# A three-block transformer kernel on one core: values made among the softmax units, head squares summed as heads come, branches of the last layer two blocks at a time

## The reference

```
# first block
x = x + 0.5 * rmsnorm(swiglu(rmsnorm(x)))
qkv = rmsnorm(x) @ w_qkv                      # 16 heads of 64: 8 "neighbourhood", 8 "dilated"
o_na, o_dil = rmsnorm(attention(...)), rmsnorm(attention(...))   # each over its 512 columns
x = x + rmsnorm(concat(o_na, o_dil) @ w_out)
x = x + 0.5 * rmsnorm(swiglu(rmsnorm(x)))
# layers l = 0, 1 (layer 0 also for a context of 256 tokens)
h = rms_norm(x) * (1 + scale) + shift          # scale, shift from (silu(c) @ w_mod + b_mod)
z = h @ w_in                                   # keys, values, forget gates, queries, branch gates
o_four, o_attn, o_hgrn = fourier(z), window_attention(z), gated_recurrence(z)   # 512 columns each
y = sum over the branches of sigmoid(gate_b) * (o_b @ w_branch_b)
x = x + m2 * (y @ w_out)
x = x + m5 * (relu(h2 @ w_ff1) ** 2 @ w_ff2)
```

## Time and profile before

| | us |
|---|---|
| median of 3 runs | 2107.01 |
| lowest, highest | 2104.97, 2107.38 |
| the profiled execution | 2112.87 |
| its span in the trace | 2111.0 |
| mean granted clock of PE in it | 0.984 |
| PE busy | 2013.7 |
| DVE, ACT, POOL busy | 1273.0, 946.5, 482.0 |

### The profile page before, as it was taken

How to read it: one execution, slowest core, us unless ns; L and a number is a source line. 1 busy time by engine, 2 the same in 40 slices (tenths; PEclk the granted TensorE clock), 3 DMA queues, 4 the chain that set the end, 5 groups by cost and what they waited for, 6 DMA issues and landing times.

```text
span 2111.0 us, 30414 instructions
## 1 busy us (share of the span) xinstructions
PE 2013.7 (95%) x12246; PEld 1761.6 (83%) x12246; DVE 1273.0 (60%) x1963; ACT 946.5 (45%) x1509; POOL 482.0 (23%) x293
## 2 busy tenths in 40 slices
PE   7999898899989999999999999999989899989999
PEld 6899876899978888787578788888878898688999
DVE  5679786578855772553864583254465946765410
ACT  5454434455447333423653442243265453655643
POOL 1201000000000000000034355455500000067887
PEclk9999998899999999999999999999999999999999
DMA  7987561366832212221023244466522333134554
GB/s 256 267 299 264 173 227 41 120 222 219 270 119 90 70 51 76 94 71 60 1 72 118 95 155 150 140 204 202 182 87 93 100 126 113 43 120 157 182 191 150
DMA packets 84636, 299.23 MB, mean 142 GB/s; under 512 B 9992, under 2 KB 13200, under 8 KB 84112
## 3 DMA queue, kind: packets, MB, share of 16 engines
q1 hardware_dynamic: 64512, 231.76, 32.4%
q0 software_dynamic: 17280, 60.95, 9.2%
q10 hardware_dynamic: 2704, 4.57, 0.6%
HBM read 296.18 MB, written 4.11 MB: 142 GB/s over the span
## 4 chain that ended last, share of the span: by engine, by line
PE 79%; DVE 9%; ACT 5%; DMA 3%; issue 3%; POOL 1%; ACTq 0%; DVEq 0%; POOLq 0%
PE ps L458 22%; PE ps L453 21%; PE ps L456 21%; DVE wl L436 3%; DMA wr<-wstream 2%; ACT wh L420 2%; PE ps L1587 1%; PE ps L538 1%; PE ps L1054 1%; PE ps L1037 1%; PE ps L981 1%; PE ps L983 1%; PE ps L986 1%; PE ps L1077 1%; PE ps L1072 1%
## 5 line engine op out<-in xcount | busy, mean ns | idle before, releaser
L453 PE MATMUL ps<-HH,wh 128*128 128x256 f32 (+1 forms) x2336 | 766.4, 328 | 27.3 <-ACT HH L1306 10.7
L458 PE MATMUL ps<-HH,wl 128*128 128x256 f32 (+1 forms) x2336 | 753.5, 323 | 6.2 <-DVE wl L436 5.3
L456 PE MATMUL ps<-HL,wh 128*128 128x256 f32 (+1 forms) x2336 | 752.7, 322 | 2.1 <-DVE HL L1320 2.0
L436 POOL TENSOR_TENSOR wl<-wr,wh 128x1024 fp32r<-128x1024 f32 x166 | 404.2, 2442 | 948.5 <-ACT wh L420 943.4
L420 ACT ACTIVATE wh<-wr 128x1024 fp32r<-128x1024 f32 x440 | 460.7, 1052 | 352.1 <-PE ps L458 291.1
L453 PEld LDWEIGHTS ps<-HH,wh 128*128 128x128 f32 x2336 | 449.5, 192 | 72.0 <-issue 28.5
L458 PEld LDWEIGHTS ps<-HH,wl 128*128 128x128 f32 x2336 | 449.2, 192 | 41.8 <-DVE wl L436 8.2
L456 PEld LDWEIGHTS ps<-HL,wh 128*128 128x128 f32 x2336 | 449.2, 192 | 38.7 <-DVE HL L1320 4.0
L436 DVE TENSOR_TENSOR wl<-wr,wh 128x1024 fp32r<-128x1024 f32 x274 | 333.4, 1225 | 227.8 <-ACT wh L420 226.4
L458 PE MATMUL ps<-HIDH,wl 128*128 128x512 f32 (+1 forms) x512 | 173.1, 338 | 0.0
L453 PE MATMUL ps<-HIDH,wh 128*128 128x512 f32 (+1 forms) x512 | 172.8, 338 | 0.0
(11 more groups left out here) (255 smaller groups left out, 2644.4 us busy)
## 6 DMA issues: line engine op xcount, KB each, us to landing
wr<-wstream SPq DMA_DIRECT2D x440, 512.0 KB, 3.4
WM<-wmod POOLq DMA_DIRECT2D x68, 512.0 KB, 3.9
X<-wmod POOLq DMA_DIRECT2D x28, 512.0 KB, 5.8
NAB<-naskew POOLq DMA_DIRECT2D x16, 128.0 KB, 12.8
dilskew<-lines POOLq DMA_DIRECT2D x1, 2048.0 KB, 21.8
DILB<-dilskew POOLq DMA_DIRECT2D x2, 1024.0 KB, 12.5
COND<-cond ACTq DMA_DIRECT2D x2, 1024.0 KB, 4.6
CT<-consts POOLq DMA_DIRECT2D x1, 1216.0 KB, 9.9
```

The source lines that it names most:

```text
L436: ins = e.tensor_tensor(self.WL[i % NSPL][:, :], self.WR[n % NRAW][:, :], self.WH[i % NSPL][:, :].bitcast(F32), ALU.subtract)
L453: e.matmul(out, wh, xh, start=i == 0, stop=False)
L456: e.matmul(out, wh, xl, start=False, stop=False)
L458: ins = e.matmul(out, wl, xh, start=False, stop=i == n_k - 1)
```

## The change

- The second half of the values, ("vr", 1), is made by `fill` in the first four iterations of the units: one step each on PE, ACT and DVE, and the two copies to `VR` in the next two. A unit waits for the half of the values that its head is in. The four modulation products that went with these steps go to the first four steps of "wo".
- ACT squares heads 8 to 13 inside the units. PE adds the first three of the four tiles of squares before "wo", the last before slice 2 instead of all four before slice 4. ACT issues its load of `cond` after the heads instead of before.
- Branches of both layers: the sigmoids of the next turn go between this turn's weight tiles, and `Y`'s halves are made within the next turn. In layer 1 a turn is two blocks: one bank of 512 columns, one product, one sum, one sigmoid and one copy for both.
- In layer 1 DVE makes the low halves of the weights in the branches, in the output projection and in the first group of the feed-forward part; POOL begins after that group.

```diff
     def dense_group(self, e, w, group, tiles, rhs, between=lambda: None):
         for i in range(8):
-            if i == 4:
+            if i == 2:
                 between()
...
     def pe_rows(self, e, w, key, name, c0, tiles, rhs):
...
             if k % 2:
                 self.W.step((key, "step", k // 2))
+                yield
 
     def dve_rows(self, e, w, key, tiles, dst, free, mod=iter(())):
         for k in range(4):
             self.make_low(e, w, "lo_dve", (key, "step", k))
             next(mod, None)
+            yield
...
+    def pe_heads_sum(self, e, w, some):
+        for i in some:
+            self.pe_sum_take(("o", 1), i)
+            self.pe_sum_add(e, w, ("o", 1), i, 4, 256)
...
         for n in range(4):
             self.act_head_high(e, w, n)
+            if n in (1, 3):
+                self.act_head_squares(e, w, 1, (n // 2,))
             yield
+        self.act_head_squares(e, w, 1, (2,))
...
+    def turns(self, l):
+        return [(2 * g, 2 * g + 1) for g in range(4)] if l else [(d,) for d in range(8)]
...
     def act_branches(self, e, w, l, T):
-        self.act_sigmoids(e, w, l, 0)
-        for d in range(8):
-            self.act_sigmoids(e, w, l, d + 1)
+        turns = self.turns(l)
+        self.act_sigmoids(e, w, l, turns[0], (0, 2, 1))
+        for n, ds in enumerate(turns):
             for br in (0, 2, 1):
-                self.make_high(e, w, (("branch", l, d, br), 0))
-            w.wait_ge(*self.c("br").at((l, d, 4)))
-            ins = e.activation(self.y_ap(l, d, 0), self.tm.item(("acc", l, d))[:, 0:T], ACT.Copy)
-            ins.then_inc(*self.c("y_hi").mark((l, d)))
+                self.make_high(e, w, *[(("branch", l, d, br), 0) for d in ds])
+                if n and br == 2:
+                    self.act_y_high(e, w, l, turns[n - 1])
+                if n + 1 < len(turns):
+                    self.act_sigmoids(e, w, l, turns[n + 1], (br,))
+        self.act_y_high(e, w, l, turns[-1])
...
     def dve_branches(self, e, w, l, T):
...
+                if l:
+                    self.make_low(e, w, "lo_dve", *[(("branch", l, d, br), 0) for d in ds])
+                w.wait_ge(*self.c("dense").at(("branch", l, ds[-1], br)))
...
+                if n and br == 2:
+                    self.dve_y_low(e, w, l, turns[n - 1])
+        self.dve_y_low(e, w, l, turns[-1])
...
     def pe_ff(self, e, w, l, T, rhs):
...
                 self.dense_group(e, w, ("ff1", l), [tile(f) for f in range(3)], rhs)
+                if l:
+                    self.W.step(("pool on", l))
...
-        for h in range(2):
-            self.pe_rows(e, w, ("vr", h), ("w_qkv", 0), 2048 + 512 * h, 2, rhs)
+        rows = [self.pe_rows(e, w, ("vr", h), ("w_qkv", 0), 2048 + 512 * h, 2, rhs) for h in range(2)]
+        for _ in rows[0]:
+            pass
         heads = self.pe_heads(e, w)
-        self.pe_units(e, w, block1_units(), self.unit_rings(1), self.b1_qk, self.b1_values(),
-                      lambda: next(heads, None))
+        self.pe_units(e, w, block1_units(), self.unit_rings(1), self.b1_qk, self.b1_values,
+                      lambda: (next(rows[1], None), next(heads, None)))
+        self.pe_heads_sum(e, w, range(3))
         self.pe_pairs(e, w, "wo", ("w_out", 0), range(8), 4, self.o_rhs(), True, True,
-                      lambda: self.pe_sum(e, w, ("o", 1), 4, 256))
+                      lambda: self.pe_heads_sum(e, w, (3,)))
...
         self.dve_pairs(e, w, "wo", range(8), 4, lambda j: self.Y[:, 2 * j:2 * j + 2, :], "mix_post_g",
-                       [self.c("x_new").at((("down", 1), 3))])
+                       [self.c("x_new").at((("down", 1), 3))], mod)
+        for _ in mod:
+            pass
...
-        self.make_low(e, w, "lo_dve", ("pool on", l))
+        if l == 0:
+            self.make_low(e, w, "lo_dve", ("pool on", l))
         self.dve_attn_halves(e, w, l, T)
         self.dve_branches(e, w, l, T)
         self.dve_add_out(e, w, ("out", l, 0), l, T, 16, True, iter(()))
-        for _ in self.dve_adaln(e, w, ("norm ff", l), l, 1, list(range(T // 256)), ("out", l, 0)):
+        for _ in self.dve_adaln(e, w, ("norm ff", l), l, 1, list(range(T // 256)), ("out", l, 0),
+                                self.low_of_group(e, w, ("ff1", l)) if l else None):
             pass
+        if l:
+            self.make_low(e, w, "lo_dve", ("pool on", l))
```

More of the change, by code:

```diff
@@ L1066, in pe_units @@
                 w.wait_ge(*self.c("u_pt").at(u.key))
[L1067 removed]
+                for x in v_there(u):
                     w.wait_ge(*x)
@@ L2098, in pe_branches @@
     def pe_branches(self, e, w, l, T):
-        for d in range(8):
-            self.tm.take(("acc", l, d))
+        for ds in self.turns(l):
+            self.tm.take(("acc", l, ds))
             for br in (0, 2, 1):
-                key = ("branch", l, d, br)
+                key = ("turn", l, ds, br)
                 self.main.take(key)
@@ L2106, in pe_branches @@
                 name = ("w_branch_2", l, br, "split" if br == 1 else None)
-                self.dense(e, w, self.main.item(key)[:, 0:T], key, name, range(4), [(128 * d, 128 * d + 128)],
-                           self.branch_rhs(l, br, T))
-    def act_sigmoids(self, e, w, l, d):
-        if d < 8:
-            for n in range(3 * d, 3 * d + 3):
-                w.wait_ge(*self.c("gate").at((l, n)))
-                self.table(e, "sigmoid")
-                e.activation(self.g_ap(l, n), self.g_ap(l, n), ACT.Sigmoid).then_inc(*self.c("sig").mark((l, n)))
+                for i, d in enumerate(ds):
+                    self.dense(e, w, self.main.item(key)[:, T * i:T * i + T], ("branch", l, d, br), name, range(4),
+                               [(128 * d, 128 * d + 128)], self.branch_rhs(l, br, T))
@@ new lines, in act_sigmoids, with act_y_high @@
+    def act_sigmoids(self, e, w, l, ds, brs):
+        for br in brs:
+            for d in ds:
+                w.wait_ge(*self.c("gate").at((l, 3 * d + br)))
+            self.table(e, "sigmoid")
+            g = self.g_of(l, ds, br)
+            e.activation(g, g, ACT.Sigmoid).then_inc(*self.c("sig").mark((l, ds, br)))
+    def act_y_high(self, e, w, l, ds):
+        w.wait_ge(*self.c("br").at((l, ds, 4)))
+        ins = e.activation(self.y_of(l, ds, 0), self.of_turn(self.tm.item(("acc", l, ds)), ds), ACT.Copy)
+        ins.then_inc(*self.c("y_hi").mark(*[(l, d) for d in ds]))
@@ L2129, in dve_branches @@
-        for d in range(8):
-            acc = self.tm.item(("acc", l, d))[:, 0:T]
+        c, turns = self.c("br"), self.turns(l)
+        for n, ds in enumerate(turns):
+            acc = self.of_turn(self.tm.item(("acc", l, ds)), ds)
             for turn, br in enumerate((0, 2, 1)):
-                key, gg = ("branch", l, d, br), self.g_ap(l, 3 * d + br)
-                w.wait_ge(*self.c("dense").at(key))
-                w.wait_ge(*self.c("sig").at((l, 3 * d + br)))
+                key, gg = ("turn", l, ds, br), self.g_of(l, ds, br)
+                if l:
+                    self.make_low(e, w, "lo_dve", *[(("branch", l, d, br), 0) for d in ds])
+                w.wait_ge(*self.c("dense").at(("branch", l, ds[-1], br)))
+                w.wait_ge(*self.c("sig").at((l, ds, br)))
+                got = self.of_turn(self.main.item(key), ds)
@@ L2173, in dve_add_out @@
             k = key + (d,)
+            if key == ("out", 1, 0):
+                self.make_low(e, w, "lo_dve", (k, 0))
             if squares:
@@ L2308, in pe_layer @@
         self.pe_units(e, w, layer_units(l), self.unit_rings(2), lambda u: self.layer_qk(l, u),
-                      [self.c("hd_cp").at(("v2", l))], fill.all)
-        self.W.step(("pool on", l))
+                      lambda u: [self.c("hd_cp").at(("v2", l))], fill.all)
+        if l == 0:
+            self.W.step(("pool on", l))
         self.pe_branches(e, w, l, T)
@@ L2352, in act @@
         self.act_pairs(e, w, "qk", range(8), 8, False)
-        for h in range(2):
-            self.act_rows(e, w, ("vr", h))
-        heads = self.act_heads(e, w)
-        self.act_units(e, w, block1_units(), self.unit_rings(1), 0, self.b1_free(), lambda: next(heads, None))
+        for _ in self.act_rows(e, w, ("vr", 0)):
+            pass
+        rows, heads = self.act_rows(e, w, ("vr", 1)), self.act_heads(e, w)
+        self.act_units(e, w, block1_units(), self.unit_rings(1), 0, self.b1_free(),
+                       lambda: (next(rows, None), next(heads, None)))
+        for _ in heads:
+            pass
+        self.act_heads_rest(e, w, self.high_of_group(e, w, "wo"))
         self.act_cond(e, w, 1)
-        self.act_heads_rest(e, w, self.high_of_group(e, w, "wo"))
         self.act_pairs(e, w, "wo", range(8), 4, True)
@@ L2385, in act_layer @@
         self.act_forget(e, w, l, 1)
-        self.act_rows(e, w, ("vh", l))
+        for _ in self.act_rows(e, w, ("vh", l)):
+            pass
         fill = Fill(self.act_gates(e, w, l, T), l)
@@ L2434, in dve @@
```

(7 more changed lines are left out.)

55 lines of the change are left out of this document (36 added, 19 removed).

## The result

The changed kernel takes 2096.37 us (median of 5 runs, 2094.94 to 2100.23); the kernel before, run beside it, 2107.01 (2104.97 to 2111.07, 5 runs). The ratio is 0.9950, 95% interval 0.9935 to 0.9965: **10.6 us faster**, where 26.2 were forecast, and above the range's end of 2092. The profiled execution took 2094.94 us, its span 2093.1. The two profiled executions lie 17.9 us apart, the medians 10.6.

What follows compares the result with a forecast made beforehand. PE, busy 2013.7 of 2111.0 us, was taken as the bound; only its waits and low clock could be won. 10.8 + 4.3 + 1.3 - 0.6 + 7.7 + 2.7 = 26.2 us gave 2080.8, range 2075 to 2092.

Steps and rivals of the forecast that it cites:

- Units of block 1: From the values' last four steps to "wo": values' steps alternating with scores let "wo" start 10.8 us earlier.
- rival A: Units of block 1: the clock falls all the same, losing 8.2 us, time 2089.0; chance 0.15.
- + 9.5 clock: Units, 306.64 to 327.32 us: low clock costs 9.5 us, won if the clock stays at 1.00.
- these 5.9: Whole kernel: the profiled execution lay 5.86 us above the median, so 5.86 was taken off the forecast 2086.7.
- Wo: "wo": slice 4 starts 4.3 us sooner, a clock that may hold wins 1.3, moved modulation products cost 0.6.
- Branches, layer 1: Layer 1's branches and projection: 66.6 us become 58.9, a gain of 7.7, bounds 5.5 and 8.4.
- rival B: Layer 1's branches: DVE is the bound, low halves queue behind products; 2084 to 2085 us, chance 0.12.
- slices 6 and 7 wait: End of layer 1's branches: projection slices 6 and 7 wait for two blocks' product, sum, copy and low half; 0.6 us.
- Norm behind it: Norm after layer 1's branches: DVE splitting removes its clash with POOL; gain 2.7 us, bounds 0.5 and 3.5.
- Layer 0: Layer 0's branches: same instructions in another order, gain 0, bounds - 1 and + 0.5 us.
- D: Whole unit stretch: the clock, once low, does not rise, so the kernel is slower, 2127 us; chance 0.04.
- E: Waits named: they are real but something later waits for the same, as SP's stream; 2107 us, chance 0.03.

Runs made afterwards that it cites:

- the second trace: The kernel before, profiled once more without an edit: span 2102.9 us instead of 2111.0; median 2104.54 us, ratio 0.9993.
- experiment 2: The kernel before with 18 unread matmuls filling PE's wait of 4.66 us ahead of the units' first transposes: 2104.30 us, 0.9991 of the kernel before.
- experiment 4: The kernel before with only the second part: squares and sums as heads come, load of cond behind the heads; 2101.37 us, 0.9983.
- experiment 3: The kernel before with only the first part: values' second half among the units, four modulation products in "wo"; 2101.73 us, 0.9984.
- experiment 9: Experiment 7's kernel with the splits of slices 4 and 5 of "wo" made earlier: 2080.14 us, 0.9881 of the kernel before.
- experiment 7: The changed kernel with DVE's low half behind the sum into X in layer 1's projection: 2088.36 us, 0.9914 of the kernel before.
- experiment 8: The changed kernel with POOL making the low halves from layer 1's projection on, not DVE: 2092.93 us, 0.9937 of the kernel before.
- experiment 10: The changed kernel once more in another series, without an edit: 2092.41 us, 0.9939 of the kernel before.
- Experiment 5: The kernel before with only the third part: both layers' branches in new order, layer 1's low halves on DVE; 2101.09 us, 0.9985.
- experiment 12: The kernel before with the first two parts of the change together, without the third: 2097.24 us, 0.9960.
- 11: Experiment 9's kernel once more in another series, without an edit: 2080.45 us, 0.9885 of the kernel before.

## Why the prediction was wrong

Two steps failed. In layer 1 the working had no term for DVE's low half ahead of the sum into X in the projection, which gives back most of the branches' gain. In the units it took 9.5 us of low clock, read in one execution, for a cost of every execution. Then 4.2 us went to low clock where the forecast had no term.

**"Units of block 1", 10.8.** Right against the trace it was made from (10.9), wrong for the kernel. The mechanism is as forecast: no wait over 0.6 ahead of the transposes, clock 1.00, rival A didn't come. The term that fails is "+ 9.5 clock": by the second trace it is 2 to 3 (5.8 us low, half of it; 2.1 by experiment 2), and the stretch gains 4.1; over the five traces that keep the wait it gains some 6 on average (123.2 to 117.1). The other terms add to 1.3 and fit both traces of before. The sign was in the numbers at hand: the profiled execution lay 5.9 above the median of the runs. The prediction took these 5.9 off the result as if they stood elsewhere; 6.9 of the 8.1 us between the two traces of before lie in the units, so they were mostly the same low clock that it had also counted as a gain.

**"Wo", 4.3 + 1.3 - 0.6.** 3.7 on the first trace, 4.6 on the second, 3.9 by experiment 4 against the second trace (34.15 to 30.26): the 4.3 holds. The 1.3 for the clock does not: after 2.10 and 0.76 it fell as after 4.96, for some 3 us (358.88 to 361.44 in steps of 0.21). The prediction let the clock hold because in its trace it had not fallen behind a wait of 2.45. The second trace of the same kernel shows it fall in that recurrence behind one of 2.05, where the first trace kept it (1662.76, wait 2.04, the 16 matmuls in 2.02):

```profile
1655.14 2.55 PE L1587 MATMUL ps<-QQ,R 128*128 128x128 f32 x16 [2.05 <-ACT R L1634]
```
The products cost about 0.4 (the root waits 0.97 where they are in "wo", in experiment 3 and after; 0.62 where they are not, in experiment 4 and before). In experiment 9, with no wait over 0.3 there, the clock holds.

**"Branches, layer 1", 7.7.** 1.5 measured; this is the step that failed by its working. The branches themselves did as told: PE 10.00 of 10.00 us busy, DVE at 8.88 and its 512-column operations at 0.69 each, so rival B did not come. The prediction counted how busy DVE is and where ACT stands still in the branches, but of the projection only that "slices 6 and 7 wait". It didn't follow the low half that was put into DVE's order ahead of the sum into X. That low half waits for ACT's high half, ACT stands in the square of the sum before, so the operations of a block no longer overlap: 0.57 + 0.33 + 1.07 + 1.15 + 0.33 = 3.45 us a block by the starts above. Without it (experiment 7) the stretch gains 73.11 - 64.97 = 8.1, about the forecast. Against the changed kernel that is 6.6 us in this stretch of the trace, and 8.0 in the medians (2096.37 to 2088.36, of two series). It is shown twice: with POOL in the projection (8) the stretch is 5.9 shorter.

**"Norm behind it", 2.7.** 2.8 and 2.4 in the table, but this is in part luck. The clash is gone, and experiment 8 brings it back. The clock falls here all the same: in the trace of after it is low for as long as before (6.8 us), but from 3.8 us ahead of the norm's first matmul on, where PE spends 2.22 of them waiting, and not from 1.2 us behind it. In experiment 10, the same code, it is low for 10.2, and this stretch takes 189.58: 1.0 less than in the second trace of before.

**Layer 0, 0.** Experiment 5 (both layers) loses nothing in the middle (1438.15), as forecast. PE has no wait in layer 0's branches before, after, or in experiment 5.

**What the forecast had no term for.** The middle is 4.2 us longer than in the second trace. PE's instructions are the same there and its waits nearly so; what differs is the granted clock, behind the third norm 0.68 instead of 1.00 over 5 us, and again near 600 and 1170. Windows of after, then of the second trace of before, at about the same places of the program:

```profile
590.00:606.00 16.00, 10.63 (x32) 7.96 (x33) 10.88 (x20) 7.51 (x15) 0.00 (x0) 0.79 0.00 0
1164.00:1176.00 12.00, 8.73 (x24) 6.03 (x23) 9.81 (x25) 8.07 (x17) 7.23 (x1) 0.72 0.22 89
```
```profile
598.10:614.10 16.00, 10.32 (x38) 7.86 (x37) 10.51 (x19) 7.57 (x14) 0.00 (x0) 0.89 0.01 5
1170.00:1182.00 12.00, 7.59 (x23) 4.93 (x23) 8.68 (x18) 6.81 (x13) 2.51 (x1) 0.86 0.45 172
```
Summed over the middle, the traces have PE at 1.2 GHz for 27.3 us after and for 17.1 in the second trace of before. The length less half of that time is 1429.0 to 1430.2 us in all fourteen traces of this case. So the 4.2 us are low clock; that is shown. In the four traces whose code is the same up to layer 1 (the changed kernel, 7, 8 and 10) this stretch is 1442.6 to 1442.8, in experiment 12 1440.4; in 9 and 11, one code, it is 1440.1 and 1438.2, and in the two traces of before 1441.7 and 1438.5. The Trainium skill, "TensorE: Matmul & The Clock Gate", Part 1, says that what gates the clock runs free of the kernel's start; that would let the same wait cost its spell of low clock in one execution and not in the next. Whether the changed kernel has the long middle more often than the one before is open: four traces point to it, but the timed runs (gains of 10.6 and 12.8 in two series, beside 9.8 in the traces) don't tell.

**The rivals.** A, B, D and E didn't come. Of C, only its 1.3 for the clock in "wo" did.

**The sum.** By the second trace of before, from 26.2 to the 9.8 between the traces: units -6.7 (10.8 to 4.1), "wo" -0.4 (5.0 to 4.6), layer 1 -6.2, norm 4 -0.3, middle -4.2, the start and norm 3 +1.5 (1.2 + 0.3): 9.9.

## What to carry to other kernels

Before an operation is put into an engine's order ahead of one whose result others wait for, write down the whole ring of a block: what it waits for, what the engine that makes it waits for, and whether that comes back to the same operation. The busy share (DVE 54% in that stretch: 7.52 of 14 us) doesn't show it. A spell of low clock read in one execution is no term of a sum: if the profiled execution lies above the median, take the excess off the gain, not off the total, and look at more than one trace (the units' spell had three lengths in five traces here). Work that waits for nothing should stand ahead of the chain that waits, also where it is only a split of weights: it won 4.7 us in "wo" here (29.48 to 24.76), and with that the clock.

## What was not expected of the hardware

- After the same wait of 4.65 us in the same code, TensorE came back to 2.4 GHz after 5.8 us in one execution and after 20.7 in another, PE being busy in both.
- The clock fell behind waits of 2.10 and 0.76 with 0.5 us of work between them, and behind 2.10 and 0.48 (experiment 4). Behind a wait of 2.05 it fell in one trace of the kernel before and not in the other. In experiment 12 it fell 0.9 us after the second had ended (356.98; matmuls go from 0.12 to 0.21 apart at 357.92), and stayed low to 361.3.
- Identical code differed by 8.1 us of span between two traces, with some 68 and 51 us at 1.2 GHz (by the mean clocks of 0.984 and 0.988); the medians of 12 and 29 runs by 2.8 (ratio 0.9993, 0.9981 to 1.0005).
